# Experts' weights in sixteen slots of 1 MB in place of eight of 2 MB

## The chip, the core and the metric

The kernel runs on one core of one Trainium2 chip. The core has a matrix engine (TensorE, "PE" in the profile), VectorE (DVE), ScalarE (ACT), GpSimd (POOL) and SyncE (SP), which here does nothing but wait on semaphores and issue DMAs; 16 DMA engines carry each transfer together. The metric is the time on the device of one execution, in microseconds (us).

## The reference

Two transformer blocks over one sequence of 256 tokens with 1024 features, all in float32. The first block (one layer: attention, a state-space mixer, then a mixture of experts) contains what is changed here. The second block has two layers of another kind, and begins with the sum that the experts leave.

```python
def _moe(h, w_router, b_router, w_gu, b_gu, w_dn, b_dn):    # 32 experts, 4 of them for each token
    ...
        gu = xb @ w_gu[e] + b_gu[e]                         # w_gu[e]: 1024 x 2048
        g, u = gu[:, :D_EXPERT], gu[:, D_EXPERT:]
        g = jnp.minimum(g, SWIGLU_LIMIT)
        u = jnp.clip(u, -SWIGLU_LIMIT, SWIGLU_LIMIT)
        act = (u + 1.0) * (g * jax.nn.sigmoid(SWIGLU_ALPHA * g))
        return act @ w_dn[e] + b_dn[e]                      # w_dn[e]: 1024 x 1024
```

Each expert has 8 MB of `w_gu` and 4 MB of `w_dn`; the 32 experts have 384 MB, and every byte of it is read once.

## The kernel before

**Slots.** On-chip memory holds eight slots of 2 MB for the experts' weights (`MOE_SLOTS`; a slot is 16 KB in each of the 128 partitions): slots 0 to 3 are the tensor `ring`, which the rest of the program uses too, slots 4 to 7 are the end of the tensor `work`. Each slot has a semaphore `slot_full`, which its transfer raises by 16, one for each DMA engine.

**Work.** The experts are taken two at a time, 16 pairs; one pass of a loop holds two pairs (`TWINS`, u = 0 and 1), and each of a pair's experts has room for 64 token rows (`CAP`). The products of the two experts go to the two halves of the same PSUM rows. A pair takes twelve slots: `("gu", u, q, e)` for q = 0 to 3, a quarter of `w_gu` (256 of its 1024 rows), and `("wd", u, half, e)`, half of `w_dn` (512 rows), for the two experts e in turn. In `Experts.load` (L449 to L460) partition p takes neighbouring rows of the matrix: two of `w_gu` (`"a (p k) n -> p (a k) n"`, a row has 8 KB) or four of `w_dn` (a row has 4 KB), so 16 KB without a break on both sides.

**Order on PE** (`Experts.products`, L548): for q = 0 to 3 wait for the two slots of the quarter, then 16 products (8 for each expert; the page counts two instructions for each, at L576); after q = 0 the turning of the gate weights (L564) and the bias rows (L568); in q = 3 the four PSUM columns are finished one after the other. Then the rows of the next pair are gathered (L356, 128x128 operands), the activations are turned (L606), the second bias is added (L617), and the two halves of `w_dn` follow, 16 products each (L628). Last comes `combine`, the sum back to the tokens (L356, 8 instructions of 128x512).

**Order on SP** (`Experts.load_weights`, L462): the names of `PAIR_SLOTS` in order; before the first of the two transfers of a quarter or half, SP waits until PE has used what stood in that slot, eight names earlier. PE tells this by `quarter_used` after q = 0, 1, 2, by `down_half` after the first half, and by the semaphores of the last PSUM columns for the rest. The eight slots are first filled while the layer's routing is still computed (`sync`, L855 to L864); the ninth transfer, a half of `w_dn` of pair 0, waits for the first quarter's products. After the experts SP goes on to the second block, whose first loads (`w_in`, L1960) take ring slots 2 and 3 when the last `w_gu` is used, the next when the last `w_dn` is used.

**Others.** GpSimd loads the bias rows of each pair (6 small DMAs). DVE does the clipping and adds up. The earliest loads of the program, four parts of `w_ada` (L824, `kpm`), move 2 MB each in runs of 8 KB: partition p takes rows p and p + 128 of a block, 2048 floats of each. Loads of `w_in` after them are 2 MB in runs of 2 KB.

Of the kernel before, what the change touches and what calls it, by code (L numbers as in the profile page):

```python
# [30 lines left out]
P = 128  # L31
# [22 lines left out]
SLOT = 4096  # L54
# [80 lines left out]
class Uses:  # L135
# [42 lines left out]
    def after(self, passes=1):  # L178
        return [b + passes * p for b, p in zip(self.base, self.per)]
# [66 lines left out]
QUARTERS = 4  # L246


def pair_slots(u):

    return [("gu", u, q, e) for q in range(QUARTERS) for e in range(2)] + [("wd", u, half, e) for half in range(2) for e in range(2)]
# [36 lines left out]
assert len(PAIR_SLOTS) % MOE_SLOTS == 0 and PAIRS % TWINS == 0  # L288
# [80 lines left out]
class Memory:  # L369


    def __init__(self, nc, ctx):
# [15 lines left out]
        self.experts_done = None  # L388
# [13 lines left out]
    def slot(self, i, *dims):  # L402
        n = int(np.prod(dims))
        ring, at = (self.ring, i * SLOT) if i < SLOTS else (self.work, WORK - (MOE_SLOTS - i) * SLOT)
        v = ring[:, at:at + n]
        return v.rearrange("p (a b) -> p a b", a=dims[0])

# [7 lines left out]
class Experts:  # L415
# [4 lines left out]
    def __init__(self, mem, sem, tag):  # L420
# [7 lines left out]
        self.down_half = sem("down_half" + tag)  # L428
        self.quarter_used = sem("quarter_used" + tag)
# [21 lines left out]
    def load(self, sp, io, S, slot, name, p):  # L451

        kind, u, part, e = name
        if kind == "wd":
            src = io["w_dn"][bass.ds(2 * p + e, 1), part * 512:part * 512 + 512, :]
            dst = slot(S.no(name), 4, 1024)
        else:
            src = io["w_gu"][bass.ds(2 * p + e, 1), part * 256:part * 256 + 256, :]
            dst = slot(S.no(name), 2, 2048)
        sp.dma_start(dst, src.rearrange("a (p k) n -> p (a k) n", p=P)).then_inc(*S.fills(*name))  # L460

    def load_weights(self, sp, io, S, B, slot, pair, it, skip=0):  # L462


        def last_use(name, it, turn):

            kind, u, part, e = name
            if kind == "gu" and part < QUARTERS - 1:
                return self.quarter_used, (it - turn) * 3 * TWINS + (3 * u + part + 1)
            if kind == "wd" and part == 0:  # L470
                return self.down_half, (it - turn) * TWINS + (u + 1)
# [4 lines left out]
        for i, name in enumerate(PAIR_SLOTS):  # L476
            if i < skip:
                continue
            if name[3] == 0:
                earlier = i - MOE_SLOTS  # L480
                sp.wait_ge(*last_use(PAIR_SLOTS[earlier], it, int(earlier < 0)))
            self.load(sp, io, S, slot, name, pair + name[1])
# [70 lines left out]
    def products(self, pe, mem, B, S, it, u):  # L553
# [65 lines left out]
        for half in range(2):  # L619
# [2114 lines left out]
```

## Time and profile before

| what | value |
|---|---|
| time, median of 3 runs | 2111.66 us (2111.12 to 2112.28) |
| the profiled execution, its own time | 2112.3 us |
| its span in the trace | 2110.6 us |
| PE busy | 1983.0 us, 94% of the span |
| DVE, ACT, POOL busy | 28%, 19%, 4% |
| read from HBM | 578.60 MB |

The span goes from the first instruction to the last; the 1.7 us between it and the execution's own time lie around it. In the page the span is cut into 40 slices of 52.8 us. The experts' stage is slices 8 to 25. A transfer "lands" when its semaphore has its full count. GB is 10^9 bytes, a slot of "2048.0 KB" is 2.097 MB by that count.

### The profile page before, as it was taken

What the parts mean: (1) busy time and instruction counts of PE and PEld (TensorE: products, weight loads), DVE (VectorE), ACT (ScalarE), POOL (GpSimd) and SP (SyncE); (2) the same over time, 40 slices, a digit from 0 to 9 for tenths busy, and PEclk for the clock granted to TensorE, in tenths of its full rate; (3) what the DMA queues carried; (4) which work ended last, traced back from release to release, by engine and by line L of the source; (5) the groups of instructions that cost most, each with busy time, mean ns of one, the idle gap of its engine ahead of it and who ended that gap; (6) DMA issues with size and microseconds to landing.
All of it is one profiled execution on the core that took longest, in us unless ns stands there. A gap on an engine that the chain in (4) does not pass through costs nothing.

```text
span 2110.6 us, 22836 instructions
## 1 busy us (share of the span) xinstructions
PE 1983.0 (94%) x9036; PEld 1139.0 (54%) x9036; DVE 597.1 (28%) x1238; ACT 406.3 (19%) x856; POOL 92.6 (4%) x166
## 2 busy tenths in 40 slices
PE   5999999999989999989899998999999999899998
PEld 2766875333333333333333333756988456668863
DVE  0387613222112112212112112541333035323311
ACT  2124222111110001111110102242212022421210
POOL 0000000000000000000000000200000011000000
PEclk9999999999999999999999999999999999999999
DMA  9666457999999999999999997152544334244431
GB/s 368 163 228 221 145 199 289 381 426 428 427 427 428 428 427 427 427 427 428 427 428 427 427 427 284 37 202 80 170 153 143 124 129 160 87 153 151 143 146 39
DMA packets 132786, 582.18 MB, mean 276 GB/s; under 512 B 9848, under 2 KB 56056, under 8 KB 106992
## 3 DMA queue, kind: packets, MB, share of 16 engines
q1 hardware_dynamic: 127648, 574.70, 68.3%
q0 software_dynamic: 5072, 6.56, 1.4%
q8 instruction: 46, 0.75, 0.1%
q14 instruction: 20, 0.16, 0.0%
HBM read 578.60 MB, written 2.62 MB: 275 GB/s over the span
## 4 chain that ended last, share of the span: by engine, by line
PE 73%; DMA 23%; issue 1%; ACT 1%; DVE 1%; SPq 0%; DVEq 0%; PEldq 0%; ACTq 0%
PE psum L356 52%; PE psum L628 11%; DMA work<-w_gu 10%; DMA ring<-w_gu 10%; PE psum L576 7%; DMA ring<-w_in 2%; DMA ring<-w_ada 1%; PE psum L2015 1%; PE psum L617 1%; PE psum L606 1%; ACT work L2310 0%; SPq L460 0%; PE psum L991 0%; ACT work L2300 0%; ACT work L1279 0%
## 5 line engine op out<-in xcount | busy, mean ns | idle before, releaser
L356 PE MATMUL psum<-normed,ring 128*128 128x256 f32 (+1 forms) x2432 | 508.9, 371 | 2.3 <-DMA ring<-w_in 2.1
L356 PEld LDWEIGHTS psum<-normed,ring 128*128 128x128 f32 x2432 | 443.6, 191 | 64.2 <-issue 5.6
L576 PE MATMUL psum<-ring,normed 128*64 128x512 f32 x1024 | 235.9, 615 | 32.2 <-DMA ring<-w_gu 32.2
L576 PE MATMUL psum<-work,normed 128*64 128x512 f32 x1024 | 234.4, 612 | 31.4 <-DMA work<-w_gu 31.4
L356 PE MATMUL psum<-ring,work 128*128 128x512 f32 x560 | 242.5, 592 | 2.7 <-DVE work L2616 2.7
L356 PE MATMUL psum<-work 128*128 128x128 f32 (+7 forms) x1184 | 189.4, 333 | 12.7 <-issue 8.4
L576 PEld LDWEIGHTS psum<-ring,normed 128*64 128x64 f32 x1024 | 81.7, 141 | 184.2 <-issue 184.2
L576 PEld LDWEIGHTS psum<-work,normed 128*64 128x64 f32 x1024 | 81.1, 140 | 182.9 <-issue 182.9
L356 PEld LDWEIGHTS psum<-work 128*128 128x128 f32 (+2 forms) x1184 | 139.2, 187 | 74.5 <-issue 61.9
L356 PEld LDWEIGHTS psum<-ring,work 128*128 128x128 f32 x560 | 105.8, 190 | 131.9 <-issue 131.8
L356 PE MATMUL psum<-ring,normed 128*128 128x512 f32 (+2 forms) x416 | 169.9, 564 | 4.4 <-issue 2.6
L356 PEld LDWEIGHTS psum<-ring,normed 128*128 128x128 f32 x416 | 76.9, 194 | 86.3 <-issue 83.4
L667 DVE TENSOR_SCALAR work<-psum 128x512 f32<-128x512 f32 x32 | 22.0, 687 | 325.9 <-PE psum L576 325.9
L628 PE MATMUL psum<-ring,normed 128*64 128x512 f32 x512 | 113.3, 595 | 0.0
L628 PE MATMUL psum<-work,normed 128*64 128x512 f32 x512 | 113.2, 594 | 0.0
L683 DVE TENSOR_TENSOR work<-psum,gain_rows 128x512 f32<-128x512 f32 x32 | 22.1, 692 | 274.6 <-PE psum L628 274.6
L641 ACT ACTIVATE work<-work 128x512 f32<-128x512 f32 x32 | 20.2, 630 | 400.0 <-DVEq L669 400.0
L2663 DVE SCALAR_TENSOR_TENSOR work<-psum,consts_sb,work 128x255 f32<-128x255 f32 x88 | 42.5, 482 | 187.5 <-ACT work L2435 185.9
L2435 ACT ACTIVATE work<-psum,consts_sb 128x256 f32<-128x256 f32 x88 | 44.9, 561 | 238.6 <-PE psum L356 238.6
L628 PEld LDWEIGHTS psum<-ring,normed 128*64 128x64 f32 x512 | 38.1, 137 | 73.4 <-issue 73.4
L628 PEld LDWEIGHTS psum<-work,normed 128*64 128x64 f32 x512 | 37.8, 137 | 73.6 <-issue 73.5
L638 ACT ACTIVATE work<-psum 128x256 f32<-128x256 f32 x16 | 6.1, 384 | 359.1 <-PE psum L564 359.1
(293 smaller groups left out, 1314.8 us busy)
## 6 DMA issues: line engine op xcount, KB each, us to landing
ring<-w_gu SPq DMA_DIRECT2D x64, 2048.0 KB, 27.3
work<-w_gu SPq DMA_DIRECT2D x64, 2048.0 KB, 27.4
ring<-w_dn SPq DMA_DIRECT2D x32, 2048.0 KB, 27.4
work<-w_dn SPq DMA_DIRECT2D x32, 2048.0 KB, 27.4
ring<-w_in SPq DMA_DIRECT2D x25, 2048.0 KB, 12.5
ring<-w_up SPq DMA_DIRECT2D x44, 1024.0 KB, 6.7
ring<-w_ada SPq DMA_DIRECT2D x12, 2048.0 KB, 11.8
ring<-w_down SPq DMA_DIRECT2D x10, 2048.0 KB, 7.7
```

What stands on the lines that cost most here:

```text
L356: return pe.matmul(out, lhsT, rhs, start=first, stop=last, **kw)
L576: ins = pe.matmul(b[r], self.hgT[:, 2 * q + k, r], ws[e][:, k, n0:n0 + 512], start=q == 0 and k == 0, stop=q == QUARTERS - 1 and k == 1, s ...
L606: ins = pe.transpose(psum[:, B.no(("aT", u, half)), i * P:(i + 1) * P], self.act[:, half].rearrange("p (n k) -> p k n", k=4)[:, i], K("ide ...
L617: pe.matmul(psum[:, B.no(("dn", u, dh))], mem.consts_rows("pair_row", 32 * dh), self.b_dn[32 * dh:32 * dh + 2, :], start=True, stop=False, ...
L628: ins = pe.matmul(psum[r, B.no(("dn", u, dh))], self.actT[:, 4 * half + k, r], ws[e][:, k, dh * 512:dh * 512 + 512], start=False, stop=hal ...
L638: act.activation(self.wT, psum[:, B.no(("sT", u)), 0:L], ACT.Copy).then_inc(*B.frees("sT", u))
L641: act.activation(self.u[:, half], self.g[:, half], ACT.Sigmoid, scale=ALPHA).then_inc(self.sig_ready, 1)
L667: dve.tensor_scalar(g, psum[:, B.no(("g", u, half))], LIMIT, None, ALU.min).then_inc(*B.frees("g", u, half))
L683: dve.tensor_tensor(self.out[:, j], psum[:, B.no(("dn", u, j))], self.mem.gain[:, j * 512:(j + 1) * 512], ALU.mult)\
L2015: ins = pe.transpose(bank(*name)[:, i * P:(i + 1) * P], b, ident)
L2435: ins = act.activation(taps[:, c % 3, part], bank("up", l, c)[:, part * L:(part + 1) * L], ACT.Identity, scale=prm(l, "ffn_w")[:, 3 * f + ...
L2663: step(STT(out=v[:, 1:], in0=u[:, 0:L - 1], scalar=fw[:, 0:1], in1=v[:, 1:], op0=ALU.mult, op1=ALU.add))
```

## The change

The eight slots become sixteen pieces (`PIECES`) of 1 MB, each half of an old slot (`Memory.piece`: 8 KB in each partition). `w_gu` is taken in eighths and `w_dn` in quarters (`DOWN_PARTS`); a pair has 24 transfers of 1 MB. Partition p still holds the same rows as before; the two eighths of an old quarter take every second row (`"a (p k) n -> k p (a n)"`), the two parts of an old half take two neighbouring rows of each four. PE waits for the two pieces of an eighth, does 8 products and raises `eighth_used`; o = 6 and 7 are waited for together and finished column by column, as q = 3 was. The gate weights and the first bias come after o = 1, which is where q = 0 ended. In `w_dn` each part is 8 products and the last part alone goes bank by bank. SP waits before each two transfers for what stood sixteen names earlier.

The pieces have semaphores of their own (`piece_full`) that start at zero. The first block's four slot semaphores are handed on to the second block, which counts on from `slots_filled`; `Uses.after` therefore counts transfers (`fills_per`) in place of uses (`per`).

```diff
@@ -176,7 +176,7 @@
         return self.free[self.at[name][0]], 1
 
     def after(self, passes=1):
-        return [b + passes * p for b, p in zip(self.base, self.per)]
+        return [b + passes * p for b, p in zip(self.base, self.fills_per)]
 
 
...
+EIGHTHS, DOWN_PARTS = 8, 4
 
 
 def pair_slots(u):
 
-    return [("gu", u, q, e) for q in range(QUARTERS) for e in range(2)] + [("wd", u, half, e) for half in range(2) for e in range(2)]
+    return [("gu", u, o, e) for o in range(EIGHTHS) for e in range(2)] + [("wd", u, m, e) for m in range(DOWN_PARTS) for e in range(2)]
 
...
@@ -404,6 +405,10 @@
         ring, at = (self.ring, i * SLOT) if i < SLOTS else (self.work, WORK - (MOE_SLOTS - i) * SLOT)
         v = ring[:, at:at + n]
         return v.rearrange("p (a b) -> p a b", a=dims[0])
+
+    def piece(self, i):
+
+        return self.slot(i // 2, 2, SLOT // 2)[:, i % 2]
 
 
...
         kind, u, part, e = name
+        dst = self.mem.piece(S.no(name))
         if kind == "wd":
-            src = io["w_dn"][bass.ds(2 * p + e, 1), part * 512:part * 512 + 512, :]
-            dst = slot(S.no(name), 4, 1024)
+            src = io["w_dn"][bass.ds(2 * p + e, 1), 512 * (part // 2):512 * (part // 2) + 512, :].rearrange("a (p m k) n -> m p (a k) n", p=P, m=2)
+            dst = dst.rearrange("p (k n) -> p k n", k=2)
         else:
-            src = io["w_gu"][bass.ds(2 * p + e, 1), part * 256:part * 256 + 256, :]
-            dst = slot(S.no(name), 2, 2048)
-        sp.dma_start(dst, src.rearrange("a (p k) n -> p (a k) n", p=P)).then_inc(*S.fills(*name))
-
-    def load_weights(self, sp, io, S, B, slot, pair, it, skip=0):
+            src = io["w_gu"][bass.ds(2 * p + e, 1), 256 * (part // 2):256 * (part // 2) + 256, :].rearrange("a (p k) n -> k p (a n)", p=P)
+        sp.dma_start(dst, src[part % 2]).then_inc(*S.fills(*name))
+
+    def load_weights(self, sp, io, S, B, pair, it, skip=0):
 
 
         def last_use(name, it, turn):
 
             kind, u, part, e = name
-            if kind == "gu" and part < QUARTERS - 1:
-                return self.quarter_used, (it - turn) * 3 * TWINS + (3 * u + part + 1)
-            if kind == "wd" and part == 0:
-                return self.down_half, (it - turn) * TWINS + (u + 1)
+            if kind == "gu" and part < EIGHTHS - 2:
+                return self.eighth_used, (it - turn) * 6 * TWINS + (6 * u + part + 1)
+            if kind == "wd" and part < DOWN_PARTS - 1:
+                return self.down_part_used, (it - turn) * 3 * TWINS + (3 * u + part + 1)
             done = ("u", u, 1) if kind == "gu" else ("dn", u, 1)
             full, n = B.ready(*done, it=it)
...
             if name[3] == 0:
-                earlier = i - MOE_SLOTS
+                earlier = i - PIECES
                 sp.wait_ge(*last_use(PAIR_SLOTS[earlier], it, int(earlier < 0)))
-            self.load(sp, io, S, slot, name, pair + name[1])
+            self.load(sp, io, S, name, pair + name[1])
 
     def load_biases(self, pool, io, B, p, it, u):
...
@@ -568,36 +573,36 @@
                 pe.matmul(psum[:, B.no(name)], mem.consts_rows("pair_row", 32 * c), self.b_gu[32 * c:32 * c + 2, :],
                           start=False, stop=False, skip_group_check=True)
 
-        def column(c, q, k, ws):
+        def pieces(kind, part):
+            for e in range(2):
+                pe.wait_ge(*S.ready(kind, u, part, e, it=it))
+            return [mem.piece(S.no((kind, u, part, e))) for e in range(2)]
+
+        def column(c, o, ws):
             b = psum[:, B.no(columns[c])]
             n0 = DE * (c % 2) + 512 * (c // 2)
             for e in range(2):
                 r = slice(e * CAP, (e + 1) * CAP)
-                ins = pe.matmul(b[r], self.hgT[:, 2 * q + k, r], ws[e][:, k, n0:n0 + 512], start=q == 0 and k == 0,
-                                stop=q == QUARTERS - 1 and k == 1, skip_group_check=True)
+                ins = pe.matmul(b[r], self.hgT[:, o, r], ws[e][:, n0:n0 + 512], start=o == 0, stop=o == EIGHTHS - 1,
+                                skip_group_check=True)
             return ins
 
-        for q in range(QUARTERS):
-            if q % 2 == 0:
-                pe.wait_ge(self.rows_ready[q // 2], it * TWINS + (u + 1))
-            ws = []
-            for e in range(2):
-                pe.wait_ge(*S.ready("gu", u, q, e, it=it))
-                ws.append(mem.slot(S.no(("gu", u, q, e)), 2, 2048))
-            if q < QUARTERS - 1:
-                for k in range(2):
-                    for c in range(4):
-                        if q == 0 and k == 0:
-                            pe.wait_ge(*B.empty(*columns[c], it=it))
-                        ins = column(c, q, k, ws)
-                ins.then_inc(self.quarter_used, 1)
-                if q == 0:
-                    weights_and_biases()
-            else:
-                for c in range(4):
-                    for k in range(2):
-                        ins = column(c, q, k, ws)
-                    ins.then_inc(*B.fills(*columns[c]))
+        for o in range(EIGHTHS - 2):
+            if o % 4 == 0:
+                pe.wait_ge(self.rows_ready[o // 4], it * TWINS + (u + 1))
+            ws = pieces("gu", o)
+            for c in range(4):
+                if o == 0:
+                    pe.wait_ge(*B.empty(*columns[c], it=it))
+                ins = column(c, o, ws)
+            ins.then_inc(self.eighth_used, 1)
+            if o == 1:
+                weights_and_biases()
+        ws = [pieces("gu", o) for o in range(EIGHTHS - 2, EIGHTHS)]
+        for c in range(4):
+            for i in range(2):
+                ins = column(c, EIGHTHS - 2 + i, ws[i])
+            ins.then_inc(*B.fills(*columns[c]))
 
         def flip(half):
...
@@ -616,21 +621,20 @@
             pe.wait_ge(*B.empty("dn", u, dh, it=it))
             pe.matmul(psum[:, B.no(("dn", u, dh))], mem.consts_rows("pair_row", 32 * dh), self.b_dn[32 * dh:32 * dh + 2, :],
                       start=True, stop=False, skip_group_check=True)
-        for half in range(2):
-            pe.wait_ge(*B.released("aT", u, half, it=it))
-            ws = []
-            for e in range(2):
-                pe.wait_ge(*S.ready("wd", u, half, e, it=it))
-                ws.append(mem.slot(S.no(("wd", u, half, e)), 4, 1024))
-            for k, dh in [(k, dh) for k in range(4) for dh in range(2)] if half == 0 else [(k, dh) for dh in range(2) for k in range(4)]:
+        for m in range(DOWN_PARTS):
+            if m % 2 == 0:
+                pe.wait_ge(*B.released("aT", u, m // 2, it=it))
+            ws = [w.rearrange("p (k n) -> p k n", k=2) for w in pieces("wd", m)]
+            last = m == DOWN_PARTS - 1
+            for k, dh in [(k, dh) for dh in range(2) for k in range(2)] if last else [(k, dh) for k in range(2) for dh in range(2)]:
                 for e in range(2):
                     r = slice(e * CAP, (e + 1) * CAP)
-                    ins = pe.matmul(psum[r, B.no(("dn", u, dh))], self.actT[:, 4 * half + k, r], ws[e][:, k, dh * 512:dh * 512 + 512],
-                                    start=False, stop=half == 1 and k == 3, skip_group_check=True)
-                if half == 1 and k == 3:
+                    ins = pe.matmul(psum[r, B.no(("dn", u, dh))], self.actT[:, 2 * m + k, r], ws[e][:, k, dh * 512:dh * 512 + 512],
+                                    start=False, stop=last and k == 1, skip_group_check=True)
+                if last and k == 1:
                     ins.then_inc(*B.fills("dn", u, dh))
-            if half == 0:
-                ins.then_inc(self.down_half, 1)
+            if not last:
+                ins.then_inc(self.down_part_used, 1)
 
     def act_part(self, act, B, psum, it, u):
...
-    slot_full = [sem(f"slot_full{b}") for b in range(MOE_SLOTS)]
+    slot_full = [sem(f"slot_full{b}") for b in range(SLOTS)]
+    piece_full = [sem(f"piece_full{b}") for b in range(PIECES)]
     B = Uses(bank_full, bank_free, front_banks())
-    S = Uses(slot_full[0:SLOTS], slot_full[0:SLOTS], front_slots(), inc=16, twice=[("win", 2)])
+    S = Uses(slot_full, slot_full, front_slots(), inc=16, twice=[("win", 2)])
     BP = Uses(bank_full, bank_free, PAIR_BANKS, base=B.after())
-    SP = Uses(slot_full, slot_full, PAIR_SLOTS, inc=16, base=S.after() + [0] * (MOE_SLOTS - SLOTS), first=2)
-
+    SP = Uses(piece_full, piece_full, PAIR_SLOTS, inc=16, first=4)
+
+    mem.slot_full, mem.slots_filled = slot_full, S.after()
     mem.experts_done = BP.ready("dn", TWINS - 1, 1, it=PAIRS // TWINS - 1)
     mem.x_part = lambda t, j: BP.released("y", TWINS - 1, t, j, it=PAIRS // TWINS - 1)
...
                 load(io["w_out"][:, 512 * j:512 * j + 512], *name)
-        for name in PAIR_SLOTS[0:2]:
-            sp.wait_ge(*slot_used(order[order.index(("wout", 0)) - 4 + SP.no(name)]))
-            X.load(sp, io, SP, slot, name, 0)
+        for name in PAIR_SLOTS[0:4]:
+            sp.wait_ge(*slot_used(order[order.index(("wout", 0)) - 4 + SP.no(name) // 2]))
+            X.load(sp, io, SP, name, 0)
         sp.wait_ge(mixed_ready, 4)
         for j in range(2):
             sp.wait_ge(*B.released("m", 10 + j))
-        for name in PAIR_SLOTS[2:6]:
-            X.load(sp, io, SP, slot, name, 0)
-        for name in PAIR_SLOTS[6:MOE_SLOTS]:
-            sp.wait_ge(*slot_used(("wout", SP.no(name))))
-            X.load(sp, io, SP, slot, name, 0)
-        X.load_weights(sp, io, SP, BP, slot, 0, 0, MOE_SLOTS)
+        for name in PAIR_SLOTS[4:12]:
+            X.load(sp, io, SP, name, 0)
+        for name in PAIR_SLOTS[12:PIECES]:
+            sp.wait_ge(*slot_used(("wout", SP.no(name) // 2)))
+            X.load(sp, io, SP, name, 0)
+        X.load_weights(sp, io, SP, BP, 0, 0, PIECES)
         with sp.Fori(1, PAIRS // TWINS) as i:
...
     LL = range(LAYERS)
     slots = [name for l in LL for name in layer_slots(l)]
     B = Uses(bank_full, bank_free, [name for l in LL for name in layer_banks(l)], first=BANKS - 1)
-    S = Uses(slot_full, slot_full, slots, inc=16, twice=[("up", l, j) for l in LL for j in range(FC // 2)], first=2)
+    S = Uses(mem.slot_full, mem.slot_full, slots, inc=16, base=mem.slots_filled,
+             twice=[("up", l, j) for l in LL for j in range(FC // 2)], first=2)
 
     act_step, dve_step, pool_step = sem("act_step_2"), sem("dve_step_2"), sem("pool_step_2")
```

## Rows read from the trace of the kernel before

**Rows 1.** The page, its span in 40 slices: DMA engines' share and GB/s.

```profile
DMA  9666457999999999999999997152544334244431
GB/s 368 163 228 221 145 199 289 381 426 428 427 427 428 428 427 427 427 427 428 427 428 427 427 427 284 37 202 80 170 153 143 124 129 160 87 153 151 143 146 39
DMA packets 132786, 582.18 MB, mean 276 GB/s; under 512 B 9848, under 2 KB 56056, under 8 KB 106992
```

**Rows 2.** DMA issues: target and source, count, size, median time to landing.

```profile
work<-w_gu SPq DMA_DIRECT2D x64, 2048.0 KB, 27.4
ring<-w_dn SPq DMA_DIRECT2D x32, 2048.0 KB, 27.4
```

**Rows 3.** Waits of PE, 400 to 1270 us: total, times, longest.

```profile
PE psum L576 <- DMA ring<-w_gu: 32.2, 20, 2.7
PE psum L576 <- DMA work<-w_gu: 31.4, 19, 2.7
```

**Rows 4.** Timeline of PE, experts' beginning: start, length, work [idle before it, what ended it].

```profile
366.35 7.09 PE L576 MATMUL psum<-ring,normed 128*64 128x512 f32 x32
...
373.74 1.14 PE L568 MATMUL psum<-work,consts_sb 2*128 2x512 f32 x8
374.81 13.95 PE L576 MATMUL psum<-work,normed 128*64 128x512 f32 x64
```

**Rows 5.** Timeline of SP's DMA queue at the same place.

```profile
373.47 0.80 SPq L460 DMA_DIRECT2D ring<-w_dn  x2
381.93 0.80 SPq L460 DMA_DIRECT2D work<-w_dn  x2
```

**Rows 6.** Windows: stretch, length, busy PE, PEld, DVE, ACT, POOL; clock, DMA, GB/s.

```profile
362.00:373.00 11.00, 10.95 (x61) 6.39 (x59) 3.23 (x11) 4.30 (x9) 0.00 (x0) 0.91 0.00 0
700.00:716.00 16.00, 15.27 (x68) 5.27 (x66) 5.08 (x13) 1.67 (x2) 1.00 (x2) 1.00 1.01 427
```

**Rows 7.** Timeline of PE, the last pair of experts.

```profile
1248.71 7.09 PE L576 MATMUL psum<-ring,normed 128*64 128x512 f32 x32 [0.75 <-DMA ring<-w_gu]
1258.49 8.71 PE L576 MATMUL psum<-ring,normed 128*64 128x512 f32 x32 [2.69 <-DMA ring<-w_gu]
1268.27 7.09 PE L576 MATMUL psum<-work,normed 128*64 128x512 f32 x32 [1.08 <-DMA work<-w_gu]
...
1281.26 7.09 PE L628 MATMUL psum<-work,normed 128*64 128x512 f32 x32
1288.17 7.04 PE L628 MATMUL psum<-ring,normed 128*64 128x512 f32 x32
1295.14 3.71 PE L356 MATMUL psum<-work 128*128 128x512 f32 x8
1303.63 1.94 PE L2015 MATMUL psum<-consts_sb,work 128*128 128x128 f32 x8 [4.79 <-issue]
```

**Rows 8.** Chain of work that ended last, 1180 to 1330 us: start, length, link.

```profile
1208.80 7.09 PE psum L576 x32
...
1236.55 31.59 DMA work<-w_gu
...
1268.27 7.09 PE psum L576 x32
```

**Rows 9.** Timeline of PE, the loads of `w_ada` in runs of 8 KB.

```profile
24.66 1.92 PE L356 MATMUL psum<-ring,small 128*32 128x512 f32 x16 [1.44 <-DMA ring<-w_ada]
29.63 3.57 PE L356 MATMUL psum<-ring,small 128*32 128x512 f32 x16 [3.05 <-DMA ring<-w_ada]
```

**Rows 10.** Windows in the loads of `w_ada` (8 KB) and of `w_in` (2 KB).

```profile
10.00:26.00 16.00, 8.39 (x64) 4.62 (x64) 1.30 (x4) 5.18 (x14) 0.00 (x0) 1.00 1.01 424
27.00:33.00 6.00, 3.37 (x16) 0.59 (x16) 0.00 (x0) 0.00 (x0) 0.00 (x0) 0.72 1.02 390
```

**Rows 11.** Window behind PE's longest idle time at the end of the stage.

```profile
1302.00:1313.00 11.00, 6.76 (x14) 3.64 (x15) 2.15 (x5) 3.00 (x8) 0.76 (x2) 0.53 0.80 301
```

**Rows 12.** Timeline of SP's DMA queue near the program's start.

```profile
21.56 2.08 SPq L824 DMA_DIRECT2D ring<-w_in  x2
23.69 7.93 SPq L842 DMA_DIRECT2D consts_sb<-consts  x1
```

More of the change, by code:

```diff
@@ L243, in pair_banks @@
             ("dn", u, 1), ("y", u, 0, 0), ("y", u, 0, 1), ("aT", u, 1), ("y", u, 1, 0), ("y", u, 1, 1)]
-QUARTERS = 4
+EIGHTHS, DOWN_PARTS = 8, 4
 def pair_slots(u):
-    return [("gu", u, q, e) for q in range(QUARTERS) for e in range(2)] + [("wd", u, half, e) for half in range(2) for e in range(2)]
+    return [("gu", u, o, e) for o in range(EIGHTHS) for e in range(2)] + [("wd", u, m, e) for m in range(DOWN_PARTS) for e in range(2)]
 PAIR_BANKS = [name for u in range(TWINS) for name in pair_banks(u)]
@@ L285, in layer_slots @@
     return s + [("up", l, j) for j in range(FC // 2)] + [("down", l, d) for d in range(DOWN_SLOTS)]
-assert len(PAIR_SLOTS) % MOE_SLOTS == 0 and PAIRS % TWINS == 0
+PIECES = 2 * MOE_SLOTS
+assert len(PAIR_SLOTS) % PIECES == 0 and PAIRS % TWINS == 0
 def col_pairs(v):
@@ L387, in __init__ @@
         self.x_ready, self.x_part = ctx.enter_context(nc.semaphore("x_ready")), None
-        self.experts_done = None
+        self.experts_done = self.slot_full = self.slots_filled = None
         self.staged_in = ctx.enter_context(nc.semaphore("staged_in"))
@@ L427, in __init__ @@
         self.down_bias_in = sem("bdn_in" + tag)
-        self.down_half = sem("down_half" + tag)
-        self.quarter_used = sem("quarter_used" + tag)
+        self.down_part_used = sem("down_part_used" + tag)
+        self.eighth_used = sem("eighth_used" + tag)
         self.zeroed = sem("zeroed" + tag)
@@ L449, in __init__, with load @@
         assert A.at <= WORK - (MOE_SLOTS - SLOTS) * SLOT
-    def load(self, sp, io, S, slot, name, p):
+    def load(self, sp, io, S, name, p):
         kind, u, part, e = name
+        dst = self.mem.piece(S.no(name))
         if kind == "wd":
-            src = io["w_dn"][bass.ds(2 * p + e, 1), part * 512:part * 512 + 512, :]
-            dst = slot(S.no(name), 4, 1024)
-        else:
-            src = io["w_gu"][bass.ds(2 * p + e, 1), part * 256:part * 256 + 256, :]
-            dst = slot(S.no(name), 2, 2048)
-        sp.dma_start(dst, src.rearrange("a (p k) n -> p (a k) n", p=P)).then_inc(*S.fills(*name))
-    def load_weights(self, sp, io, S, B, slot, pair, it, skip=0):
+            src = io["w_dn"][bass.ds(2 * p + e, 1), 512 * (part // 2):512 * (part // 2) + 512, :].rearrange("a (p m k) n -> m p (a k) n", p=P, m=2)
+            dst = dst.rearrange("p (k n) -> p k n", k=2)
+        else:
+            src = io["w_gu"][bass.ds(2 * p + e, 1), 256 * (part // 2):256 * (part // 2) + 256, :].rearrange("a (p k) n -> k p (a n)", p=P)
+        sp.dma_start(dst, src[part % 2]).then_inc(*S.fills(*name))
+    def load_weights(self, sp, io, S, B, pair, it, skip=0):
         def last_use(name, it, turn):
             kind, u, part, e = name
-            if kind == "gu" and part < QUARTERS - 1:
-                return self.quarter_used, (it - turn) * 3 * TWINS + (3 * u + part + 1)
-            if kind == "wd" and part == 0:
-                return self.down_half, (it - turn) * TWINS + (u + 1)
+            if kind == "gu" and part < EIGHTHS - 2:
+                return self.eighth_used, (it - turn) * 6 * TWINS + (6 * u + part + 1)
+            if kind == "wd" and part < DOWN_PARTS - 1:
+                return self.down_part_used, (it - turn) * 3 * TWINS + (3 * u + part + 1)
             done = ("u", u, 1) if kind == "gu" else ("dn", u, 1)
@@ L860, in sync @@
             sp.wait_ge(*B.released("m", 10 + j))
-        for name in PAIR_SLOTS[2:6]:
-            X.load(sp, io, SP, slot, name, 0)
-        for name in PAIR_SLOTS[6:MOE_SLOTS]:
-            sp.wait_ge(*slot_used(("wout", SP.no(name))))
-            X.load(sp, io, SP, slot, name, 0)
-        X.load_weights(sp, io, SP, BP, slot, 0, 0, MOE_SLOTS)
+        for name in PAIR_SLOTS[4:12]:
[4 more added lines that the diff above has]
+        X.load_weights(sp, io, SP, BP, 0, 0, PIECES)
         with sp.Fori(1, PAIRS // TWINS) as i:
-            X.load_weights(sp, io, SP, BP, slot, i * TWINS, i)
+            X.load_weights(sp, io, SP, BP, i * TWINS, i)
         with sp.If(X.more_rounds(sp)):
@@ L871, in sync @@
                 with sp.Fori(0, PAIRS // TWINS) as i:
-                    X.load_weights(sp, io, SP, BP, slot, i * TWINS, r * (PAIRS // TWINS) + i)
+                    X.load_weights(sp, io, SP, BP, i * TWINS, r * (PAIRS // TWINS) + i)
             sp.wait_ge(*BP.ready("dn", TWINS - 1, 1, it=ROUNDS * (PAIRS // TWINS) - 1))
@@ L1842, in second_block @@
     bank_free = [sem(f"bank_free_2_{b}") for b in range(BANKS)]
-    slot_full = [sem(f"slot_full_2_{b}") for b in range(SLOTS)]
     LL = range(LAYERS)
```

## The prediction

> **What bounds the kernel now.** I read the page's slices first. In the experts' stage the DMA engines are at 9 tenths or more and the GB/s stand at 427 or 428 slice after slice [rows 1]. That is a ceiling and not a coincidence of demand: a load of experts' weights takes 27.4 us from issue to landing [rows 2], while two of them (4.19 MB) land within 9.78 us (below), so five or six are always queued. PE's waits come second: 39 of them, 63.6 us together, none over 2.7 us, all for `w_gu` [rows 3]. The timeline of PE shows the rhythm: the last three quarters of a pair begin at 1248.71, 1258.49 and 1268.27, which is 9.78 us apart, or **4.89 us for 2 MB**, while a quarter's products take 7.09 us [rows 7]. PE is faster than the loads and waits for them. The chain of waits repeats a link "DMA" of 31.59 us in every pair, and one pair's last quarter follows the other's after 1268.27 - 1208.80 = 59.47 us [rows 8], of which twelve loads are 58.7. The 0.8 us left over I put down to the small bias loads, which the change doesn't touch.
>
> The stage therefore begins when the DMA engines start again. They stand still first: in 362 to 373 us they move nothing [rows 6], because all eight slots are full and SP waits for the products of the first quarter. These run from 366.35 to 373.44 [rows 4], and SP issues at 373.47 [rows 5]. Of the 192 loads 8 are there by then, and 4 (the last `w_dn`) come after the last `w_gu`. So **180 loads** lie between 373.47 and 1268.27: 180 x 4.89 = 880 us, plus 0.8 for each of 15 further pairs is 892, against 894.8 seen. The account closes to 3 us, which is about what a first load needs beyond its 4.89.
>
> Behind the last `w_gu` PE is not waiting: q = 3 (7.09), turning and gathering to 1281.26, `w_dn` 14 us, `combine` to 1298.9, then the second block [rows 7]. What moves the landing of the last `w_gu` moves the end.
>
> **Part 1: the DMA engines start earlier.** The first pieces are free after 8 products in place of 16: half of 7.09 us, at about 369.9 in place of 373.47. Does the queue then run dry? Two pieces are 4.9 us of transfer; the next two are free at 373.44, 3.5 us later; the next two follow after the gate weights and bias (1.1 us and a bit [rows 4]) and another 3.5, at about 378.4, when 9.8 us have been given out at 373.4. It does not run dry. Gain: **-3.5 us**, whole, as long as the loads bound all the rest.
>
> **Part 2: shorter runs.** This is the term that decides. A partition's share of a transfer is now one run of 8 KB where it was 16 KB. The page says what a packet is: of 132,786 packets 106,992 are under 8 KB, so at most 25,794 are larger; 403 MB in runs of 8 KB would be 49,152 packets, in runs of 16 KB 24,576 [rows 1]. So it was 16 KB, and the change adds 24,576 packets, 8 per engine for each 2 MB. The trace has the same transfer in runs of 8 KB, in the loads of `w_ada`: with their queue full, two of them land 29.63 - 24.66 = **4.97 us** apart [rows 9]. That is 0.08 us more than 4.89. Windows support it with less resolution: 424 GB/s there, 427 in the experts, 390 in runs of 2 KB [rows 6, 10]. 2.097 MB at 390 GB/s is 5.38 us, 0.49 more than 4.89 for 56 more packets on each engine: 8.7 ns per packet, so 8 of them are 0.07 us. Two independent readings give 0.07 and 0.08 us; I take 0.075: 180 x 0.075 = **+13.5 us**. Bounds: from the windows alone, 2.097/424 - 2.097/427 is 0.035 us, +6.3 us; from the landings alone, +14.4 us.
>
> The Trainium skill has a rule on this in "DMA: Bandwidth & Descriptors", section "Why small descriptors are slow (HBM only)": about 3 bus cycles are lost per packet. With the 850 MHz of its section on where 436 GB/s comes from that is an estimate of 3.5 ns per packet, 8 x 3.5 x 180 = 5.1 us in all. The rows of `w_ada` and `w_in` say 8.7 to 10 ns, over twice that: the trace disagrees.
>
> **Part 3: twice as many transfers.** Each transfer ends in a completion on every engine, and there is one more per 2 MB. No row shows one alone; it can't well cost more than a packet (8.7 ns, 180 x 0.0087 = 1.6 us) nor less than nothing. I take +0.8. SP issues two loads in 0.80 us [rows 5], so 24 per pair are 9.6 of 59.5 us, and only later loads of the same queue stand behind them. SP has once been held for 7.93 us when long queues of short runs stood ahead [rows 12]; twelve or thirteen pieces of 8 packets per engine are about 100, fewer than the two 64-packet `w_in` loads there, and a full queue would not idle the engines anyway. Nothing.
>
> The same page, "Measured" under Bandwidth, gives single DMAs of 1 MB 341 GB/s and a fixed 2.0 us, and advises larger ones. Taken one by one, 192 further transfers would cost 384 us, an estimate. The trace disagrees for queued loads: 4.89 us for 2 MB at 428 GB/s leaves no room for a fixed cost.
>
> **Part 4: PE's waits are gathered in one place.** More waits on PE cost nothing: 64 products' instructions cross a quarter's border, with two waits, in 13.95 us, less than twice 7.09 [rows 4]. But o = 6 and 7 still wait for all of the old quarter, as q = 3 did, so nothing is gained at the last `w_gu`. Ahead of it o = 5 lands four pieces earlier, 9.9 us, and needs 3.5: PE then stands still for about 6.4 us in one piece, where it had waits of up to 2.7. After a wait of 2.69 us a quarter took 8.71 us in place of 7.09 [rows 7], at the lower of the two clocks (1.2 in place of 2.4 GHz) for a part. In most pairs that is hidden (PE has 6 us to spare). In the last pair it is exposed, and the quarter had run there at full speed: **+1.6 us**. Bounds: 0, and 5 us, from the window after the idle 4.79 us, where the clock was 0.53 for 11 us (11 x 0.47) [rows 7, 11].
>
> **The rest.** The `w_dn` pieces of the last pair land 5, 10, 15 and 20 us after the last `w_gu` and are needed 13, 16.5, 20 and 23.5 us after it (1281.26 - 1268.27 = 13.0): no wait, where the second half now is needed 19.9 us and lands 19.6 us after. PSUM bank 0 of `w_dn` is full 1.8 us before the end in place of 3.5, and DVE's step on it takes 0.7: still hidden. Slots 2 and 3 of the ring are free for the second block at the same point. The own semaphores and the counting of `after` move no instruction; where the old count was one transfer low (slot 2), the wait for the other expert's load, issued later on the same queue, stood right behind.
>
> **Sum.** -3.5 + 13.5 + 0.8 + 1.6 = +12.4 us. On the profiled execution: 2112.3 + 12.4 = 2124.7. The median of the runs lies 0.6 below that execution, so I forecast **2124.1 us**. Its own range is 2114.5 (6.3 for the runs, nothing for completions and clock) to 2129.2 (14.4, 1.6 and 5): an increase of 2.8 to 17.5.
>
> **Rivals.**
> - *Packets cost nothing in this stage*, because the two eighths of an old quarter read neighbouring memory, unlike `w_ada`. For it: the windows differ by 0.7% only. Against: the landings, and 390 GB/s for 2 KB. It ends at -3.5 + 1.6, 2109.8 us: not slower. It decides if a packet costs under 2.4 ns (3.5 / (8 x 180)). Chance 0.07.
> - *A packet costs half as much here*, as the windows alone have it: 0.035 us in 8 packets or 4.4 ns, a landing distance of 4.93 us, -3.5 + 6.3 + 1.6 = +4.4, 2116.1 us or a little under, at the border of what can be measured. For it: a window counts bytes, not the slowest engine. Against: it rests on 3 GB/s. Chance 0.08. The Trainium skill's rule above lies nearest to this rival; by its estimate the sum would be -3.5 + 5.1 + 1.6 = +3.2.
> - *The pairs' extra 0.8 us goes with the smaller transfers*, since the bias loads find gaps among them: 15 x 0.8 = 12 us back, against 13.5 lost; with the earlier start 2112 or less, and faster by 10 if packets are cheap too. The trace shows no such gap in any stretch. Chance 0.04.
> - *The low clock stays on*, and PE with some 53 us of work and 5 more at half speed comes near the 60 of a pair, and the exposed tail pays in full: 2128 to 2140. Chance 0.06.
> - *Every second 8 KB loads memory unevenly*: were the rate that of the short runs, 390 GB/s, 180 x 0.49 = 88 us. `w_in`'s strided runs show no such effect beyond their packets. Chance 0.02.
>
> The forecast itself has 0.73. About 0.2% (4.2 us) is what a measurement of this kernel can tell from no change: within it lie the first rival, half of the second, a part of the third and the lowest edge of the forecast, 0.14; faster 0.03; slower 0.83. The range of 8 in 10 reaches down past the second rival and up past the forecast's upper edge: 2113.5 to 2130.
>
> **What would show it.** Landings of the last quarters 9.93 to 9.98 us apart per 4.19 MB (9.78 would refute part 2); 24,576 packets more, at or over 8 KB; windows of 420 to 424 GB/s; SP's first refill at 369.9; an idle time of PE of about 6.4 us before o = 6 of each pair; the last `w_gu` waited for until about 1279. The forecast is wrong if the distance stays at 4.89, or if the engines idle between loads.

## The result, and the profile after

| | before | after |
|---|---|---|
| median | 2111.39 us (4 runs, 2110.83 to 2112.28) | 2127.28 us (4 runs, 2126.19 to 2128.37) |
| profiled execution, span | 2112.3, 2110.6 | 2126.46, 2124.8 |
| ratio | | 1.0072, 95% interval 1.006 to 1.0084 |

The change makes the kernel slower by 15.9 us (12.7 to 17.7 by the interval). 2124.1 was forecast, in a range of 2113.5 to 2130. Where the executions of a kernel fell into a faster and a slower group (`e4_parts64` alone, below), its ratio is that of the faster one.

The page of the changed kernel, its slices and packets, answers to [rows 1]:

```profile
DMA  9566357999999999999999997052544334244431
GB/s 371 159 227 227 133 198 302 420 420 421 421 421 421 421 420 421 421 420 421 421 420 421 421 420 286 12 211 78 181 144 144 135 129 158 80 157 144 144 149 40
DMA packets 160436, 582.21 MB, mean 274 GB/s; under 512 B 12920, under 2 KB 59128, under 8 KB 110064
```

The stage's ceiling is 420 or 421 GB/s in place of 427 or 428. There are 27,650 packets more: 24,578 of them of 8 KB and over (160,436 - 110,064 less 25,794) and 3,072 of under 512 B, which is 16 for each of the 192 further transfers: one completion for each DMA engine would give this number.

Next the timeline of PE of the changed kernel: the first products, then the last two pairs and the second block's beginning; the refill on SP's queue stands in a fence of its own. Columns as in [rows 4, 5, 7].

```profile
364.53 7.09 PE L586 MATMUL psum<-ring,normed 128*64 128x512 f32 x32
...
1215.59 8.72 PE L586 MATMUL psum<-ring,normed 128*64 128x512 f32 x32 [4.66 <-DMA ring<-w_gu]
...
1256.18 13.95 PE L586 MATMUL psum<-ring,normed 128*64 128x512 f32 x64
1275.94 9.26 PE L586 MATMUL psum<-work,normed 128*64 128x512 f32 x32 [5.81 <-DMA work<-w_gu]
...
1304.98 3.71 PE L357 MATMUL psum<-work 128*128 128x512 f32 x8
1313.60 0.87 PE L2021 MATMUL psum<-consts_sb,work 128*128 128x128 f32 x3 [4.91 <-issue]
1319.54 1.33 PE L2021 MATMUL psum<-consts_sb,work 128*128 128x128 f32 x5 [5.07 <-issue]
1321.77 12.01 PE L357 MATMUL psum<-ring,normed 128*128 128x512 f32 x24 [0.90 <-issue]
```

```profile
368.22 4.24 SPq L465 DMA_DIRECT2D ring<-w_dn  x4
```

One pair's last quarter follows the other's after 1275.94 - 1215.59 = 60.35 us, where [rows 8] give 59.47: 0.88 us more for twelve loads' worth of data, 0.073 us for each 2 MB.

The account of the two profiled executions, interval by interval:

| interval | before | after | difference |
|---|---|---|---|
| start to the first product of the experts | 366.35 | 364.53 | -1.8 |
| first product to first refill | 7.12 | 3.69 | -3.4 |
| first refill to the last quarter's products | 894.80 | 907.72 | +12.9 |
| these to `combine` | 26.87 | 29.04 | +2.2 |
| `combine` to the first transposes | 8.49 | 8.62 | +0.1 |
| these to the next eight (1321.02, 1333.61) | 17.39 | 20.01 | +2.6 |
| the rest of the span | 789.58 | 791.19 | +1.6 |

### The profile page after: what moved, and what is told of

Same layout as the page of the kernel before. It is cut to its first block, busy times and chain, and to the rows that moved or that the text cites. A ratio compares the mean times of both kernels' runs of the same rounds, so it can differ in the third digit from the quotient of the medians.

```text
span 2124.8 us, 23505 instructions
## 1 busy us (share of the span) xinstructions
PE 1986.8 (94%) x9036; PEld 1126.3 (53%) x9036; DVE 597.0 (28%) x1238; ACT 406.3 (19%) x856; POOL 92.8 (4%) x166
## 2 busy tenths in 40 slices
DMA packets 160436, 582.21 MB, mean 274 GB/s; under 512 B 12920, under 2 KB 59128, under 8 KB 110064
## 4 chain that ended last, share of the span: by engine, by line
PE 72%; DMA 19%; SPq 5%; issue 2%; ACT 1%; DVE 1%; DVEq 0%; PEldq 0%; ACTq 0%
PE psum L357 52%; PE psum L586 10%; DMA work<-w_gu 9%; PE psum L632 8%; DMA ring<-w_gu 7%; SPq L465 5%; DMA ring<-w_in 2%; DMA ring<-w_ada 1%; PE psum L2021 1%; PE psum L622 1%; PE psum L611 1%; ACT work L2316 0%; PE psum L997 0%; ACT work L2306 0%; ACT work L1285 0%
## 5 line engine op out<-in xcount | busy, mean ns | idle before, releaser
L586 PE MATMUL psum<-work,normed 128*64 128x512 f32 x1024 | 239.6, 626 | 38.5 <-DMA work<-w_gu 38.5
L357 PE MATMUL psum<-work 128*128 128x128 f32 (+7 forms) x1184 | 191.2, 337 | 12.7 <-issue 8.4
L586 PEld LDWEIGHTS psum<-work,normed 128*64 128x64 f32 x1024 | 77.0, 144 | 198.9 <-issue 198.8
L586 PEld LDWEIGHTS psum<-ring,normed 128*64 128x64 f32 x1024 | 76.2, 143 | 191.0 <-issue 191.0
L632 PE MATMUL psum<-work,normed 128*64 128x512 f32 x512 | 113.0, 594 | 0.0
L632 PEld LDWEIGHTS psum<-ring,normed 128*64 128x64 f32 x512 | 36.1, 137 | 74.6 <-issue 74.6
L632 PEld LDWEIGHTS psum<-work,normed 128*64 128x64 f32 x512 | 36.1, 137 | 74.6 <-issue 74.6
## 6 DMA issues: line engine op xcount, KB each, us to landing
ring<-w_in SPq DMA_DIRECT2D x25, 2048.0 KB, 12.4
```

Source lines behind the costliest of these rows:

```text
L357: return pe.matmul(out, lhsT, rhs, start=first, stop=last, **kw)
L586: ins = pe.matmul(b[r], self.hgT[:, o, r], ws[e][:, n0:n0 + 512], start=o == 0, stop=o == EIGHTHS - 1, skip_group_check=True)
L632: ins = pe.matmul(psum[r, B.no(("dn", u, dh))], self.actT[:, 2 * m + k, r], ws[e][:, k, dh * 512:dh * 512 + 512], start=False, stop=last a ...
```

## The experiments

Medians of 5 runs (4 or 6 where said), each beside the kernel before on the same chip. Ratios are to that. The edits are cut to the lines that matter, and some of these are shortened; of `e1`, `e2` only the patterns are shown, without the code around them.

**1. Longer or shorter runs alone** (`e1_runs8`, `e2_runs4`).

```diff
 # e1: w_gu (w_dn: "a (m p k) n -> p (a m) (k n)", m=2)
-"a (p k) n -> p (a k) n"
+"a (k p) n -> p (a k) n"
 # e2: w_gu seen as rows of 1024 floats, then both matrices alike; slot viewed as 4 x 1024
+"a r (h n) -> a (r h) n", then "a (k p) n -> p (a k) n"
```

> The kernel before with one thing changed: each of its 192 transfers of 2 MB takes its rows so that every partition gets two runs of 8 KB in place of one of 16 KB (rows p and p + 128 of w_gu, two blocks of w_dn). The features of the weights then don't match those of the activations, so the output is not the reference's; slots, semaphores and the number of transfers and products are those of before. Theory (8 further packets per engine and transfer at some 9 ns): transfers land 4.97 us apart in place of 4.89, 180 x 0.075 to 0.08, so 13.5 to 14.5 us slower than before, about 2125.3. Rival, the loss comes from the number of transfers or from the slots: within 2 us of before, and 4.89 us. Rival, half the price per packet: +6, 4.93 us.

Measured 2128.11 us against 2111.44, +16.7, ratio 1.0082 (1.0069 to 1.0095).

> The kernel before with each 2 MB transfer in runs of 4 KB (four per partition; the features of weights and activations don't match, so the output is not the reference's), 24 further packets per engine and transfer. Theory, a fixed cost per packet of 9.3 ns: a landing distance of 4.89 + 0.22 = 5.11 us, 180 x 0.22 = 40 us slower than before, about 2152; it falls on the line through runs of 16, 8 and 2 KB. Rival, the loss at 8 KB is one step (memory read in two passes, or a path that 16 KB runs alone take): about the 16 us of the first experiment again.

Measured 2153.98 us (4 runs) against 2112.87, +41.1, ratio 1.0196 (1.0181 to 1.0212). The last quarters' landings in PE's timeline, first with runs of 8 KB, then of 4 KB:

```profile
1270.15 7.09 PE L576 MATMUL psum<-ring,normed 128*64 128x512 f32 x32 [1.16 <-DMA ring<-w_gu]
1280.07 8.78 PE L576 MATMUL psum<-work,normed 128*64 128x512 f32 x32 [2.83 <-DMA work<-w_gu]
```

```profile
1296.01 7.09 PE L575 MATMUL psum<-ring,normed 128*64 128x512 f32 x32 [1.45 <-DMA ring<-w_gu]
1306.25 8.78 PE L575 MATMUL psum<-work,normed 128*64 128x512 f32 x32 [3.15 <-DMA work<-w_gu]
```

That is 9.92 and 10.24 us for 4.19 MB: 4.96 and 5.12 us for 2 MB, where [rows 7] have 4.89. Over 8 and 24 further packets per engine the rise is 0.07 and 0.23 us, or 9 to 10 ns for each. The slots, the semaphores, PE's order and the number of transfers are those of before in both. A single step at 8 KB is out. Why `e1_runs8` takes 16.7 and not 13.5: from its refill at 372.00 to 1280.07 there are 13.3 us more than before, its last quarter fell to the low clock too (8.78 in place of 7.09, above), and some 2 us more lie behind `combine`. That its total is close to the changed kernel's is in part chance: it has no earlier refill (3.4 us), and the changed kernel loses most of that again in its last quarter and behind it.

**2. More transfers, with the run length changed and without** (`e3_halves8`, `e4_parts64`).

```diff
 # e3 (src split into the same two runs of 8 KB as in the changed kernel)
+for m in range(2):                      # runs of 8 KB
+    sp.dma_start(dst[:, m], src[m]).then_inc(*S.fills(*name))
 # e4
+for m in range(2):                      # runs of 16 KB, 64 partitions each
+    sp.dma_start(dst[64*m:64*m+64], src[64*m:64*m+64]).then_inc(*S.fills(*name))
```

> The kernel before, each slot of 2 MB filled by two transfers of 1 MB in runs of 8 KB, both counted by the slot's one semaphore; full computation. SP's waits and PE's order stay those of before. Theory: what the first experiment gives, and 192 further completions at 0 to 9 ns on each engine: 0 to 1.6 us above it, so 13.5 to 16 us above before; landing distance of a full slot 4.97 to 4.98 us. Rival, each transfer has a fixed cost of its own that a full queue doesn't hide: well over 2 us above the first experiment.

Measured 2127.04 us, ratio 1.0074 (1.0061 to 1.0087): 1.1 us below `e1_runs8`. The traces tell it more sharply: from the first refill to the last quarter's products there are 908.13 us here (371.81 to 1279.94) and 908.07 there, so in a full queue 192 further transfers cost nothing that can be seen.

> The kernel before, each slot of 2 MB filled by two transfers of 1 MB over 64 partitions each, in runs of 16 KB as before; full computation. It doubles the number of transfers and leaves the run length. Theory: 0 to 1.6 us slower than before (192 completions), landing distance 4.89 to 4.90 us. Rival, the number of transfers is what costs: about the 13 us of the first experiment.

Measured 2872.16, 2893.96 and 2902.98 us, and 3047.20 to 3048.64 in three more executions; ratio 1.365 (1.361 to 1.3695). Theory and rival both missed it by some 760 us. Its window against the one of [rows 6]:

```profile
700.00:716.00 16.00, 9.50 (x32) 3.11 (x32) 0.00 (x0) 0.00 (x0) 0.00 (x0) 0.68 1.00 225
```

The DMA engines are busy all the time and move 225 GB/s, about half. Its page has 135,860 packets, 25,796 of them of 8 KB and over, so the runs are still 16 KB. So loads over half the partitions, with the other half's load queued right behind, moved about half of what loads over all 128 move. What halves the rate no run here shows. This is why the experiment can't serve as the test of the number of transfers that it was meant to be; `e3_halves8` is that test.

**3. The early refill** (`e6_late_free`, with the changed kernel again as `e8_after_again`).

```diff
-return self.eighth_used, (it - turn) * 6 * TWINS + (6 * u + part + 1)
+return self.eighth_used, (it - turn) * 6 * TWINS + (6 * u + part // 2 * 2 + 2)
-if kind == "wd" and part < DOWN_PARTS - 1:
-    return self.down_part_used, (it - turn) * 3 * TWINS + (3 * u + part + 1)
+if kind == "wd" and part < 2:
+    return self.down_part_used, (it - turn) * 3 * TWINS + (3 * u + 2)
```

> The changed kernel with SP waiting for both eighths of an old quarter (and both parts of an old half of w_dn) before it loads into either: the finer slots stay, their earlier refill goes. Theory (the earlier refill is worth 3.5 us once, at the stage's beginning): 3.5 us slower than the changed kernel, about 2130.8; the first refill 7.1 us after the first product in place of 3.7. Rival, the earlier refill is worth nothing, because the kernel before with 1 MB transfers and coarse refill took 2127.0, the changed kernel's time: 2127.3.

> The changed kernel once more, to compare the others of this call with on the same chip: 2126 to 2128.5, 15.9 us above before.

Measured 2131.37 (2129.81 to 2137.39) and 2128.14 us (2126.34 to 2134.66): 3.2 us between the medians, which the spread of the runs alone would not settle. The traces do: the first refill comes 7.13 and 3.69 us after the first product (373.31 for 366.18, 369.88 for 366.19), and from there to the last quarter's products both take the same, 907.90 and 907.81 us (to 1281.21 and 1277.69). The 3.4 us of the start are kept to the end, as worked out.

**4. PE's gathered wait** (`e7_seventh_at_once`).

```diff
...                                     # last_use: one more eighth in the count
-for o in range(EIGHTHS - 2):
+for o in range(EIGHTHS - 1):
...
-ws = [pieces("gu", o) for o in range(EIGHTHS - 2, EIGHTHS)]
+ws = pieces("gu", EIGHTHS - 1)          # and one product per column and expert behind it
```

> The changed kernel with the products of o = 6 done as soon as their pieces are there, and those of o = 7 alone column by column. Theory: behind the last landing only 8 products remain in place of 16 (-3.5 us), and PE's idle time ahead of them falls from some 5.8 to 1.4 us, so the clock stays up and the 2.2 us that the last quarter lost by it come back: 2121.6, still 10 above before. Rival, the stage's end doesn't follow the last w_gu but the w_dn that lands up to 20 us behind it: -0 to -2 us, about 2126.

Measured 2122.12 us, 6.0 below `e8_after_again` (5.7 expected). The last two eighths of its last pair, in PE's timeline:

```profile
1272.93 3.65 PE L586 MATMUL psum<-work,normed 128*64 128x512 f32 x16 [1.32 <-DMA work<-w_gu]
1277.89 3.65 PE L586 MATMUL psum<-work,normed 128*64 128x512 f32 x16 [1.31 <-DMA work<-w_gu]
```

Waits of 1.3 us in place of one of 5.8, and 3.65 us of products behind the last landing in place of 9.26. The landings 1277.89 - 1272.93 = 4.96 us apart, for two pieces of 1 MB, give the landing distance for 2 MB with the small pieces. The finer slots had this gain in them, and the changed kernel left it.

**5. The gap in the second block's transposes** (`e10_hold_loads`).

```diff
 if i == 2:
     sp.wait_ge(*mem.experts_done)
+    sp.wait_ge(*B.ready("nT", 0, 0, 0, 1))
```

> The changed kernel with the second block's third and fourth w_in loads held back until PE has done the first eight transposes of that block. Theory (PE stands still for 5 us behind its third transpose because its next instructions come by DMA and queue behind these loads): the eight transposes run without the gap, 3 to 5 us faster than the changed kernel, about 2124. Rival, the gap has nothing to do with the loads (clock, a wait of PE that the profile doesn't name): it stays, 2127 to 2128, or slower if the held loads are late for their own products.

Measured 2122.80 us against 2111.69, ratio 1.0046 (1.0029 to 1.0062), where the changed kernel had +15.9 and +15.3: 4 to 5 us gained. PE's timeline:

```profile
1315.06 0.90 PE L2022 MATMUL psum<-consts_sb,work 128*128 128x128 f32 x3 [3.55 <-ACT work L2338]
1316.38 1.33 PE L2022 MATMUL psum<-consts_sb,work 128*128 128x128 f32 x5 [0.41 <-issue]
```

The gap of 5.07 us is 0.41, and the idle time ahead of the first transposes is 3.55 us in place of 4.91. From `combine` (1307.81 here) to the first transposes there are 7.25 us in place of 8.62, from these to the next eight (1331.61) 16.55 in place of 20.01: together 4.8 us. Both depend on the loads issued just ahead of them.

The trace also shows what may have waited behind the loads. One DMA queue, q8, carries packets of the kind "instruction", 16 KB each. Shares of the DMA queues in 1306.90 to 1308.10 us of the kernel before, then in 1316.90 to 1318.10 us of the changed one:

```profile
q8 instruction: 1, 0.02, 5.8%
```

```profile
q8 instruction: 1, 0.02, 6.2%
```

PE goes on at 1309.37 and 1319.54, behind these. The packet ahead of each lies in 1300.9 to 1302.1 and 1310.9 to 1312.0 us, and PE begins the transposes at 1303.63 and 1313.60. In every profile with such a gap PE goes on 1.2 to 1.7 us after the packet. With the loads held back (`e10_hold_loads`) the second packet starts 3.2 us after the first, where the other two kernels have 6.0. That these packets are PE's own program is inferred from this fixed distance; the trace doesn't name the engine of the queue.

It also tells why the changed kernel loses more. The second packet ends 12.9 us after `combine` begins in the kernel before, 13.1 in the changed one, so at nearly the same time. But PE stops at another place of its program: before it has 23 instructions left until the next eight transposes (11.65 us), in the changed kernel five transposes, a pause of 0.90 us and 24 instructions (14.07 us). That is 2.4 of the 2.6 us in the account.

**6. The bias loads** (`e5_bias_once`, then as full computations `e9_biases_ahead` and `e11_ahead_hold`).

```diff
 # e5: the loop over pairs goes; PE waits for the constants 64 and 32
+X.load_biases(pool, io, BP, 0, 0, 0)
 # e9: all experts' rows at once, picked by a selector that DVE makes for each pair
+pool.dma_start(self.b_gu[32*c:32*c+32, :], io["b_gu"][:, n0:n0 + 512])
+dve.tensor_scalar(self.pair_rows[:, u], K("pair_row"), K("pair_no")[:, bass.ds(e2, 1)], None, ALU.is_equal)
+pe.matmul(psum[...], self.pair_rows[32*c:32*c+32, u], self.b_gu[32*c:32*c+32, :], ...)
 # e11: e9 and the wait of experiment 5
```

> The kernel before with the experts' biases loaded for the first pair alone and used for all pairs (the output is therefore not the reference's): 90 of the 96 small loads by GpSimd are gone. Theory (the 0.8 us by which a pair's period of 59.47 exceeds twelve loads is what these small transfers take from one or two engines): the period falls to 58.7 and the end comes 15 x 0.8 = 12 us earlier, about 2099.5. Rival, the 0.8 us has another source (the loop, SP's issues, the slots): no change beyond 1 us, period still 59.4.

Measured 2101.83 us against 2111.44, ratio 0.9953 (0.994 to 0.9965). From the first refill (371.17) to the last quarter's products there are 886.24 us in place of 894.80, so the stage is 8.6 us shorter. One pair's last quarter follows the other's after 1257.41 - 1198.64 = 58.77 us, where [rows 8] give 59.47:

```profile
1198.64 7.09 PE L576 MATMUL psum<-ring,normed 128*64 128x512 f32 x32 [2.71 <-DMA ring<-w_gu]
...
1257.41 7.09 PE L576 MATMUL psum<-work,normed 128*64 128x512 f32 x32 [2.70 <-DMA work<-w_gu]
```

> The kernel before (eight slots, runs of 16 KB), full computation, with the biases of all 32 experts loaded once, ahead of the first pair, by six transfers over 32 partitions each; the bias rows' products take 32 rows in place of 2, with a selector that DVE builds for each pair (some 0.2 us of DVE per pair). Theory: what loading them once gave, 9.6 us faster than before, about 2102.5; a pair's period 58.7 to 58.8. Rival, DVE's step delays the gathering of a pair or the six loads the first one: less than half of that gain.

> Both together on the kernel before: biases ahead, and the two w_in loads held back; full computation. Theory: 9.6 us from the biases and 2 us from the gap of 0.9 and 1.7 us behind the first product of the second block: about 2100. Rival, the second part gives nothing where the gap is short: 2102.5.

Measured 2103.45 and 2100.82 us against 2111.69, ratios 0.9956 (0.994 to 0.9972) and 0.9942 (0.9928 to 0.9956). `e11_ahead_hold` beats both kernels: eight slots of 2 MB with runs of 16 KB, six bias loads in place of 96, and the second block's next loads kept back for a moment. The 2.6 us between it and `e9_biases_ahead` lie inside the spread of the runs (2101.08 to 2106.05 and 2100.23 to 2102.92).

## Why the prediction was right, and where it was short

- **What bounds the kernel**: right. Runs of 8 KB in otherwise the same kernel lengthen the stage by 13.3 us, where the changed kernel's is longer by 12.9. The 0.8 us by which a pair exceeded twelve loads were rightly put down to the bias loads: without them 0.70 of it goes (`e5_bias_once`).
- **Part 1, the early refill, -3.5 us**: 3.4 in the account, 3.2 between `e6_late_free` and `e8_after_again`.
- **Parts 2 and 3, +13.5 and +0.8**: 12.9 in the account, 13.3 for `e1_runs8`; the 14.3 of the sum were 1.4 too much. The landing distance is 4.96, read from `w_ada` as 4.97, and the price per packet of 9 to 10 ns holds for a third run length. The 390 GB/s for 2 KB were read in a window that has the end of `w_ada` in it (its last part lands at 29.63); 29.70 to 33.00 us has 387, which gives 9.4 ns per packet in place of 8.7. The 0.8 for completions was too much: `e3_halves8` shows none. The rivals with cheap packets (4.89 and 4.93 us) are refuted, and so are the one with unevenly loaded memory and the one in which a pair's extra 0.8 us goes: 60.35 us are twelve times 4.96 and 0.83. The Trainium skill's 3 bus cycles per packet ("DMA: Bandwidth & Descriptors", "Why small descriptors are slow (HBM only)"), 3.5 ns by estimate, are about a third of what the runs show. The Trainium skill's fixed 2.0 us stands in another section than the prediction has it, "Anatomy of one DMA — SWDGE (gpsimd) path", for DMAs that GpSimd issues; for the loads here, which SP issues into a full queue, 192 more of them cost nothing (908.13 against 908.07 us).
- **SP's issues**, put at 0.4 us each and 9.6 us per pair, were mis-sized, though it cost nothing. In the changed kernel SP stands at an issue for a median of 1.5 to 1.9 us (least, median and longest in ns):

```profile
L465 SPq DMA_DIRECT2D ring<-w_gu x128: 327/1493/5917, 305.7 to 1238.1; - x128
```

  By these medians 24 issues would be some 40 of a pair's 60 us, an estimate. The DMA engines stayed full all the same (420 GB/s from 368.22 to 1275.94 us).
- **Part 4, the gathered wait, +1.6**: 2.2. The wait came as worked out, 5.81 us against 6.4, and the quarter behind it took 9.26 us in place of 7.09. `e7_seventh_at_once` undid it. The length of one wait doesn't settle the clock: after 2.69 us a quarter took 8.71 [rows 7], after 2.71 and 2.70 in `e5_bias_once` 7.09. Some executions reached the times of the rival in which the low clock costs more (2128 to 2140): two of the four of the changed kernel took 2128.09 and 2128.37, but at the mean clock of the other two (0.972 against 0.973); one of `e8_after_again` took 2134.66, at 0.969 against 0.972. No trace shows that one, so whether the clock made it slow stays open.
- **"The rest", where the second block was to follow unchanged**: this is the term that the sum lacked, put at nothing. The sum was 3.5 us short of the medians (12.4 against 15.9), and 2.6 us are the gap among the first transposes. These were counted as following the experts by a fixed distance; the rows already had idle times with the releaser "issue" there, but 4.79 us alone was looked at. Kernels made from the one before have the eight transposes in one piece and shorter gaps behind, or none; those made from the changed one stop after the third. `e10_hold_loads` ties the gap to the loads. Another 1.6 us are the rest of the span, which holds two stretches at the lower clock between 1330 and 2100 us where the profile of before has one (mean 0.83 in 1434 to 1444 and in 1833 to 1843 us of the changed kernel, the second below; before only in 1422 to 1432). `e7_seventh_at_once` and `e10_hold_loads`, made from the changed kernel, have one such stretch there, and their rest takes 789.51 and 789.49 us, as before's 789.58. So the 1.6 us go with the clock of an execution, and nothing ties them to the change.
- **Luck**: what was too much (1.4 us in parts 2 and 3) and what was missing (0.6 in part 4, 2.6 and 1.6 behind the stage) partly cancel. With parts 2 and 3 exact the sum would have been +11.0 us, 4.9 short of the medians in place of 3.5.
- **Open**: -1.8 us ahead of the experts, where nothing was changed. The first products began between 364.05 and 366.85 us in the eleven profiles with the same work in front of them, so the -1.8 is an execution's own variation. That the two profiled executions differ by 14.2 and the medians by 15.9 fits that. Why a stretch at the lower clock comes in one execution and not in another is open too.

```profile
1833.00:1843.00 10.00, 7.07 (x48) 6.25 (x49) 5.43 (x10) 6.16 (x17) 0.00 (x0) 0.83 0.29 95
```

## What to carry to other kernels

In a stage whose DMA engines are always busy, as this one, a finer slot bought only what happens once, at the stage's two ends, and paid with every packet that its shorter runs added: 3.4 us against 13. Look for a stretch of the trace that already moves data in the run length you plan, and read the landing distance there; it was right to 0.01 us. If a slot is made finer, use it at the last landing too: products that still wait for the old group give that gain away.

## What was not expected of the hardware

- Loads over 64 partitions, two for each slot and all queued, moved 225 GB/s with the DMA engines busy all the time, against 427 for loads over 128.
- Ninety small loads of 4 KB, 0.37 MB in all, cost 9.6 us by the medians; in the profiles the stage, which moves 403 MB, is 8.6 us shorter without them. They lengthen a pair's period by 0.7 us, while the stage shows 427 GB/s with and without them. Over 894.80 and 886.24 us that makes about 382 and 378 MB, where the 180 loads that landed are 377.5. So with the small loads more was moved than had landed, as if some DMA engines ran ahead while a landing waits for the last one; the traces don't tell the engines apart.
- PE can stand still for 5 us without a semaphore, behind loads of data: while these were queued, a packet of 16 KB of instructions came 6.0 us after the one ahead of it in place of 3.2.
